# Where ScalarE computes the gelu of four expert values: place 6 or place 8 of its group

## The reference

```
q     = (xb @ w_q)                      # 8 heads, two halves of 128
sc    = q . sub_keys                    # 128 scores for each half
eidx  = 16 best of the 16 x 16 sums     # 16 experts for each token and head
g     = softmax(top_s)
hid   = gelu(einsum('thkd,td->thk', u_tab[eidx], xb)) * g
out   = einsum('thk,thkd->td', hid, v_tab[eidx])
```

## Time and profile before

| what | value |
|---|---|
| time, median of 3 executions | 1612.42 us (1608.67 to 1612.79) |
| the profiled execution's own time | 1613.89 us |
| its span, from first to last instruction | 1611.9 us |
| busy PE, DVE, POOL, ACT | 1270.3, 1157.3, 781.3, 431.8 us |
| bytes gathered | 536.91 MB |
| mean granted TensorE clock | 0.910 |

### The profile page before, as it was taken

How to read it: one execution, slowest core, us unless ns; L and a number is a source line. 1 busy time by engine, 2 the same in 40 slices (tenths; PEclk the granted TensorE clock), 3 DMA queues, 4 the chain that set the end, 5 groups by cost and what they waited for, 6 DMA issues and landing times.

```text
span 1611.9 us, 12702 instructions
## 1 busy us (share of the span) xinstructions
PE 1270.3 (79%) x3523; PEld 651.6 (40%) x3523; DVE 1157.3 (72%) x2781; ACT 431.8 (27%) x1046; POOL 781.3 (48%) x650
## 2 busy tenths in 40 slices
PE   7976999898857995777787877778787777777776
PEld 6645565565333663333333333223333333333332
DVE  2237878999999887866676677666667776676753
ACT  3323223444434212222222222222222222222221
POOL 0005646765556765444444444545445454444540
PEclk9988998897778997999989998998989999999998
DMA  9449988998769999999999999999999999999992
GB/s 354 155 174 355 348 308 321 335 347 327 248 229 359 351 407 348 424 421 422 421 422 421 421 421 423 421 422 421 422 421 421 422 406 422 421 422 421 421 421 118
DMA packets 101324, 594.90 MB, mean 369 GB/s; under 512 B 11656, under 2 KB 11656, under 8 KB 45832
## 3 DMA queue, kind: packets, MB, share of 16 engines
q0 software_dynamic: 92160, 536.91, 82.9%
q1 hardware_dynamic: 9096, 57.19, 9.2%
HBM read 591.96 MB, written 2.10 MB: 369 GB/s over the span
## 4 chain that ended last, share of the span: by engine, by line
DMA 28%; PE 19%; DVE 17%; ACT 2%; issue 2%; POOL 0%; POOLq 0%; DVEq 0%
PE acc L819 13%; DMA act_mem<-in_peer_uv_dram,eidx 12%; DMA v_ring<-in_peer_uv_dram,eidx 9%; DMA map_mem<-in_peer_uv_dram,eidx 8%; PE mm L652 4%; DVE act_mem L1303 2%; DVE map_mem L1303 2%; DVE v_ring L1303 2%; PE acc L652 2%; DVE v_all L1303 1%; DVE u_ring L1303 1%; DVE onehot L1270 1%; DVE w_ring L1303 1%; DVE onehot L1263 1%; DVE picked L1274 1%
## 5 line engine op out<-in xcount | busy, mean ns | idle before, releaser
L572 POOL DMA_INDIRECT u_ring<-in_peer_u_dram,eidx x128 | 157.0, 1227 | 215.7 <-DVE gneg L1280 113.6
L983 ACT ACTIVATE gel<-hid 128x4 f32<-128x4 f32 x128 | 26.2, 205 | 770.1 <-DVE hid L1303 721.7
L819 PE MATMUL acc<-v_all,diag 128*128 128x512 f32 x256 | 143.2, 712 | 89.7 <-ACT diag L990 89.7
L819 PE MATMUL acc<-w_ring,diag 128*128 128x512 f32 x256 | 138.6, 692 | 76.4 <-ACT diag L990 76.4
L579 POOL DMA_INDIRECT v_ring<-in_peer_v_dram,eidx x128 | 154.7, 1209 | 84.9 <-DVE h L1319 52.0
L819 PE MATMUL acc<-u_ring,diag 128*128 128x512 f32 x256 | 134.8, 676 | 72.8 <-ACT diag L990 72.8
L1319 DVE SCALAR_TENSOR_TENSOR h<-v_ring,coef,h 128x1024 f32<-128x1024 f32 x128 | 164.3, 1284 | 4.5 <-issue 1.1
L1295 DVE CUSTOM_DVE_ANT_0 u_ring<-u_ring,hn 128x1024 f32<-128x1024 f32 x128 | 156.3, 1221 | 7.0 <-DMA u_ring<-in_peer_u_dram,eidx 5.0
L593 POOL DMA_INDIRECT u_ring<-in_peer_uv_dram,eidx x64 | 78.7, 1230 | 132.9 <-PE acc L819 116.4
L593 POOL DMA_INDIRECT v_all<-in_peer_uv_dram,eidx x64 | 78.0, 1219 | 133.1 <-PE acc L819 130.1
L593 POOL DMA_INDIRECT w_ring<-in_peer_uv_dram,eidx x64 | 74.5, 1164 | 128.8 <-PE acc L819 127.0
(11 more groups left out here) (217 smaller groups left out, 2210.4 us busy)
## 6 DMA issues: line engine op xcount, KB each, us to landing
w_ring<-in_slabs_dram SPq DMA_DIRECT2D x38, 1024.0 KB
v_ring<-in_slabs_dram SPq DMA_DIRECT2D x6, 1024.0 KB, 8.2
u_ring<-in_slabs_dram SPq DMA_DIRECT2D x4, 1024.0 KB, 9.6
h<-in_x_dram SPq DMA_DIRECT2D x4, 512.0 KB, 7.1
u_ring<-in_peer_u_dram,eidx POOLq DMA_INDIRECT x128
v_ring<-in_peer_v_dram,eidx POOLq DMA_INDIRECT x128
out_dram<-fin SPq DMA_DIRECT2D x4, 512.0 KB, 8.0
subkT<-in_sub_cols_dram SPq DMA_DIRECT2D x1, 1024.0 KB, 8.3
```

Of the source, the lines that this page charges most:

```text
L572: nc.gpsimd.indirect_dma_start(out=u_ring[:, c % U_RING, :], out_offset=None, in_=peer_u[0], in_offset=bass.IndirectOffsetOnAxis(ap=eidx[n ...
L819: last = nc.tensor.matmul(acc[half][:, :], diag[:, c % COLS, :], v_row(n, c)[:, half * BANK:(half + 1) * BANK], start=(n % PH == 0 and c = ...
L983: nc.scalar.activation(gel[:, par, g0:g0 + COLS], hid[:, par, g0:g0 + COLS], ACT.Gelu).then_inc(gelu_done, 1)
```

## The change

In tile 0 ScalarE issued the gelu of a group ahead of the pieces of place 6 (2 * COLS - 2). Now it issues it ahead of the pieces of place 8 (2 * COLS), the last one, so behind the pieces of places 6 and 7. DVE's, PE's, POOL's and SP's orders are as they were. So is the place of the table loads by rule: directly before the activation that needs one.

```
                     for gap in range(GAPS):
-                        if gap == 2 * COLS - 2:
+                        if gap == 2 * COLS:
                             gelu(n, n % 2, grp * COLS)
                         for p_ in pieces_in(n, grp, gap):
                             piece(*p_)
```

## The result

| | before | after |
|---|---|---|
| median of 13 runs | 1609.95 us (1604.14 to 1612.79) | 1614.09 us (1609.66 to 1616.0) |
| ratio to before | | 1.0031, 95% interval 1.0021 to 1.0041 |
| the profiled execution's own time | 1613.89 us | 1609.66 us |

By the medians the change costs 4.1 us, by the ratio 5.0 us (3.4 to 6.6). The two profiled executions stand the other way round: that of before is 3.9 us above the median and longer than all 13 timed ones, that of after is the shortest of its 13. So times are taken from the ratio, and the profiles are compared piece by piece only.

What follows compares the result with a forecast made beforehand. DMA bounds from 626 us, but starts after DVE's last add of tile 0; before, PE, DVE, then PE set the pace. -0.8 + 0.6 + 1.0 + 1.0 = +1.8 on 1612.4 gives 1614.2 us, range 1607.0 to 1619.5.

Steps and rivals of the forecast that it cites:

- nothing at all: Rival for the whole kernel: every term hidden, 1612.4 us; chance 0.70 together with the forecast.
- Front, -0.8: Groups 0 and 1: root 1.1 us earlier, table reload at the next root gives 0.3 back; gain 0.8 us.
- Groups 3 and 4, hidden: Late gelus make DVE about 5.2 us late, covered by its 7.86 us wait at the forget gates; cost 0.
- Attention, +0.6: Groups 7 to 21: a few gelus come 0.2 to 0.5 us late for DVE's coefficients; cost 0.6 us.
- PE's waits pay: Rival, attention: PE's starts held by a waiting gelu set the pace; up to 8.4 us faster, 1605.8; chance 0.12.
- Group 22, +1.0: Copy of the transposes comes 1.5 us later, so PE's output projection loses 1.0 and DVE waits; cost 1.0 us.
- Gain 0: Attention: PE no longer waits behind the gelu (3.45 us in group 21), which was said to bring nothing.
- Queries and end, +1.0: Groups 24 to 31: 5.0 us slip absorbed by waits; last gelu 2.1 late less PE's gain of 1.1; cost 1.0.
- Whatever moves DVE's last add moves the end: End of tile 0: the last stage's fifth gather waits for that add, so the end moves by as much.
- a lost cover: Rival, queries: the 5.0 us slip isn't made good and DVE reaches the last gelu late; 1619.2 us, chance 0.15.
- Dearer switches: Rival: a table load right after a copy or exp costs about double its 1.28 us; 1620.6 us, chance 0.03.
- the fifth gather 1.8 us later: Sign at the last stage's start: POOL's fifth gather, which waits for DVE's last add, about 1.8 us after 626.58.

Runs made afterwards that it cites:

- g21_22: Against the kernel before, only the gelus of groups 21 and 22 issued at place 8 instead of 6; ratio 1.0013 (0.9998 to 1.0029).
- only_7_21: Against the kernel before, only the gelus of groups 7 to 21 (attention) issued at place 8 instead of 6; ratio 1.0019 (1.0006 to 1.0033).
- the three early ones: Kernel before with gelus issued earlier instead of later: group 31; groups 25 to 28, 30 and 31; or groups 30 and 31. Ratios 1.0007, 0.9982, 0.9991.
- only_24_31: Against the kernel before, only the gelus of groups 24 to 31 (queries) issued at place 8 instead of 6; ratio 1.0015 (0.9997 to 1.0033).
- early_31: Against the kernel before, only group 31's gelu moved, earlier, to place 4 ahead of query 15's copy; ratio 1.0007 (0.9994 to 1.0019).
- only_22: Against the kernel before, only group 22's gelu issued at place 8 instead of 6; ratio 1.0008 (0.9993 to 1.0022).
- g0_27: Against the kernel before, only the gelus of groups 0 and 27 issued at place 8 instead of 6; ratio 1.0002 (0.9990 to 1.0013).
- all but 21: The changed kernel with group 21's gelu put back to place 6; ratio to the kernel before 1.0021 (1.0006 to 1.0036).
- all but both: The changed kernel with the gelus of groups 21 and 22 put back to place 6; ratio to the kernel before 1.0006 (0.9992 to 1.0019).
- all but 22: The changed kernel with group 22's gelu put back to place 6; ratio to the kernel before 1.0030 (1.0018 to 1.0042).

## Why the forecast came out as it did

The forecast was no change that can be told, 1.8 us slower. Measured was slower in the same direction, 4.1 to 5.0 us, at the edge of the 4.8 us that the forecast took for what can be told. A ratio of 1 lies outside the measured interval, so the rival *nothing at all* is ruled out. The measured 1614.09 us is inside the range, but its nearness to the forecast 1614.2 is luck: the forecast started from a median of three, 1612.4, which lies 2.5 us above the median of 13, and put too little on top. Step by step:

**Front, -0.8: mechanism right, size off.** From query 8's copy (at 125.66 us, before at 128.35) to the root it took 3.72 instead of 4.86 us: 1.1 earlier, as forecast. The reload at the second root was to give back 0.3. It gave back all: DVE waits 0.79 us for that root, and from the first root to DVE's reciprocal of the second it is 142.47 - 129.38 = 13.09 us, where the earlier trace rows have 12.03. The forecast had taken the 1.0 us by which DVE came late to that root for slack; but DVE too is earlier now, there 16.02 us behind the copy (142.47 - 0.79 = 141.68) instead of 16.89. From the copy to the forget gates before took 86.88 and after 86.94 us. So 0.

**Groups 3 and 4, hidden: right to 0.1 us.** Late by 5.23 (5.1 forecast), hidden by a wait that shrank from 7.86 to 2.69.

**Attention, +0.6: not told.** The new small waits are there (0.4 in group 13, 0.3 in group 18). In the table, the five kernels that move these groups take 271.2 us on the mean and the nine others (`g21_22`, which moves one of them, included) 272.9, but the nine alone go from 270.7 to 276.3. A gain of 1.7 us, the rival "PE's waits pay" in a small size, is as possible as none; the time of `only_7_21`, which is longer than before, speaks against it.

**Group 22, +1.0: the step that was mis-sized.** "PE loses 1.0" is right for group 22 by itself (29.32 for 28.31 us). What failed is "Gain 0" for group 21: an earlier PE is no nought but a cost, because it stands idle all the longer ahead of the transposes, and behind that idle time its clock was lower. With both moved the projection piece takes 3.5 us more. Putting the two back takes the 3.5 us away in the profile and brings the ratio from 1.0031 to 1.0006. The two intervals (1.0021 to 1.0041 and 0.9992 to 1.0019) don't meet, so that the pair costs time is shown; its size in time, 4.0 us by the two ratios, is known to some 3 us only. In the profiles it is the largest single term.

**Queries and end, +1.0: right in place, too small.** The slip of 5.0 us (4.55 measured) is taken up, as forecast, and query 7 starts behind the keys. But I took the catching up as free. DVE gets back 4.55 us by passing waits, and the transfers, busy all the while (share 1.01 from 560 to 600 us), don't get faster with it: DVE then waits for rows, 5.0 us for u and 2.3 for v between 520 and 612. With groups 24 to 31 moved the piece takes 434.6 us on the mean of five kernels; without, 432.8 on the mean of six (the three early ones left out): +1.8 us. Of that 1.4 us falls behind `hn` (323.55 against 322.17 us to the next). Four of the five have late first rows there, as with groups 24 to 31 alone:

```profile
628.70 1.23 DVE L1304 CUSTOM_DVE_ANT_0 map_mem<-map_mem,hn 128x1024 f32<-128x1024 f32 x1 [0.53 <-DMA map_mem<-in_peer_uv_dram,eidx]
631.19 1.23 DVE L1304 CUSTOM_DVE_ANT_0 map_mem<-map_mem,hn 128x1024 f32<-128x1024 f32 x1 [1.25 <-DMA map_mem<-in_peer_uv_dram,eidx]
```

The profile of after is the exception: no late row, 322.19 us behind `hn`, and 0.5 us in the whole piece. The first gather tells them apart: it went out 100.3 us after tile 1's last norm2 in after, and 101.4 to 103.0 in the other four, with 1.4 to 3.0 us in the piece. So 1.8 is a mean of unlike executions, and the time of `only_24_31` (2.4 us, -0.5 to 5.3) doesn't settle it.

**"Whatever moves DVE's last add moves the end": wrong as a rule.** It overlooks the four gathers ahead of the fifth. `early_31` moved `hn` by 5.8 us and the end by nothing that can be told (1.1 us slower, -1.0 to 3.1).

**The sum.** 0 + 3.5 + 1.8 = 5.3 us with attention at nothing, 3.6 with it at -1.7; measured 5.0 (3.4 to 6.6). With the 0.5 of after's own profile for the queries it is 4.0 and 2.3. Of the rivals, "a lost cover" came in small part at most: the slip at the forget gates was hidden whole, and of the 5.0 in the queries no more than the 1.8 came through. "Dearer switches" is refuted: the load at 617.22 follows a copy at once and ends at 618.50, and the gelu starts at 618.51; so at 526.57, with its gelu at 527.86. The Trainium skill (page "ScalarE: Activation LUTs", section "What ACT_TABLE_LOAD costs") adds 1.38 us of drain to each switch; these rows show none.

**What was forecast of the profile.** Right: the root 1.1 us earlier, coefficients about 5 us late in groups 4 and 25, the forget gates' wait down to "about 2" (2.7), ACT's waits for the fourth dot down from 47.0 to 10.4 us, query 7. Wrong: DVE's waits for the gelu "some 26" (20.1; its own terms give 19.4 + 10.1 - 8.8 = 20.7 and the smaller new ones), and the fifth gather 1.8 us later (1.2 earlier in this execution, since the attention part was 2.6 us shorter).

**Open.** What attention itself gains or loses, within 2 us; and why the part behind the second `hn` takes some 662 us in a few profiled executions (before, `only_22`, `g0_27`) and 659 to 660 in the others. It doesn't go by what was moved, and it is most of why the profile of before lies above its median.

## What to carry to other kernels

An engine that is let run ahead isn't a gain of nought: look at where it stands still next, and what comes late there. Before a slip is written off against later waits, look at whether the transfers can follow the catching up. And where a stage begins, list every transfer in the queue ahead of the one that waits last: an earlier end pays only if all of them go out earlier too.

## What the runs showed of the hardware

A microsecond or three of idle time ahead of 8 matmuls cost 1.5 to 3.0 us in the matmuls themselves: 1.0 us more of it (all but 21 against all but both) cost them 1.7 us, 3.2 us more cost them 1.5 in one kernel (groups 7 to 21 alone) and 3.0 in another (all but 22), both against before. They took 3.67 us in nine of the fourteen kernels, with a clock of 1.00 in each, and 5.14 to 6.64 us, with a clock of 0.71 down to 0.55, in the five others of the table above. More idle time wasn't always dearer (3.21 and 1.23 us gave 6.64, 3.21 and 2.26 gave 6.12). And 2.26 us in one piece, with none ahead of the transposes, cost nothing. The 16 matmuls behind them took 7.03 us in before, in after and in the kernels that leave out 21, 22 or both, at a clock of 1.00 in after.
